# All four channel tiles of a width-31 convolution as packed matmuls, and the memory's transposes one at a time

## The reference

```python
h = rmsnorm(x, mix_pre_norm)
u = h @ w_in                             # 1024 -> 3072
u_a, u_b, hq, hk, hv, hg = six parts of 512 columns of u
# conformer_conv: 512 channels, each with its own 31 taps back in time
c = u_a * sigmoid(u_b)
y = depthwise_conv(c, dw_w) + dw_b       # y[t, ch] = sum_w c[t - 30 + w, ch] * dw_w[w, ch] + dw_b[ch]
y_conv = silu(layernorm(y, ln_w, ln_b))  # mean and variance over the 512 channels
# retention: 4 heads of 128, chunks of 128 tokens, rotary on q and k, decay
y_ret = silu(hg) * rmsnorm_per_head(retention(rotary(hq), rotary(hk), hv))
x = x + rmsnorm(concat(y_conv, y_ret) @ w_out, mix_post_norm)
# then a gated feed-forward of width 2816, a gate on a projected input p, and the second block
```

## Time and profile before

| | |
|---|---|
| profiled execution | 929.86 us |
| its span | 928.0 us |
| granted TensorE clock, mean | 0.994 |
| TensorE busy | 901.5 us, 97% |
| its weight loads (beside the matmuls) | 813.9 us, 88% |
| VectorE busy | 663.8 us, 72% |
| ScalarE busy | 506.1 us, 55% |
| GpSimd busy | 304.7 us, 33% |
| moved by DMA | 163.77 MB, mean 176 GB/s |

### The profile page before, as it was taken

The page is one execution under the profiler, slowest core; times in us unless marked ns, Lnnn a source line. Parts: engine busy times, 40 slices in busy tenths (PEclk is TensorE's granted clock), DMA queues, the critical chain, the costliest instruction groups (busy, mean ns, idle before and its releaser), DMA issues.

```text
span 928.0 us, 16426 instructions
## 1 busy us (share of the span) xinstructions
PE 901.5 (97%) x6864; PEld 813.9 (88%) x6864; DVE 663.8 (72%) x834; ACT 506.1 (55%) x746; POOL 304.7 (33%) x115
## 2 busy tenths in 40 slices
PE   7998999999999999999999999999999999999996
PEld 6998986888888878999999998999999788888885
DVE  4999576888884256758878774867656689999622
ACT  6544736554454446755636575555545466666532
POOL 2000000566664420000000004845684156566542
PEclk9999999999999999999999999999999999999999
DMA  9583453655555545445544434533455365555551
GB/s 355 214 252 112 145 208 119 230 192 193 191 182 186 198 160 181 171 153 196 208 138 156 160 100 156 183 137 132 141 188 199 101 240 181 189 194 201 189 181 45
DMA packets 31800, 163.77 MB, mean 176 GB/s; under 512 B 9169, under 2 KB 10977, under 8 KB 13296
## 3 DMA queue, kind: packets, MB, share of 16 engines
q1 hardware_dynamic: 31664, 162.66, 51.0%
q0 software_dynamic: 64, 0.08, 0.0%
HBM read 161.32 MB, written 1.42 MB: 175 GB/s over the span
## 4 chain that ended last, share of the span: by engine, by line
PE 82%; DVE 13%; ACT 3%; issue 1%; DMA 1%; SPq 0%; DVEq 0%; ACTq 0%
PE ring L1629 28%; PE acc L1707 18%; PE acc L1641 9%; PE ring L1641 9%; PE acc L1642 4%; PE ring L1642 4%; DVE w_lo L1079 3%; PE ring L1660 3%; DVE conv_y L1171 3%; PE acc L1887 1%; DVE y L1131 1%; DVE ret_inv L1245 1%; ACT sq L679 1%; DMA gain_mix_pre<-gains 1%; ACT w_hi L673 1%
## 5 line engine op out<-in xcount | busy, mean ns | idle before, releaser
L636 POOL TENSOR_TENSOR w_lo<-raw,w_hi 128x1024 fp32r<-128x1024 f32 x100 | 287.3, 2875 | 590.8 <-ACT w_hi L673 590.7
L673 ACT CAST w_hi<-raw 128x1024 fp32r<-128x1024 f32 x284 | 297.8, 1054 | 314.7 <-PE ring L1629 132.5
L1079 DVE TENSOR_TENSOR w_lo<-raw,w_hi 128x1024 fp32r<-128x1024 f32 x184 | 228.6, 1256 | 107.5 <-ACT w_hi L673 97.4
L1629 PE MATMUL ring<-h,w_hi 128*128 128x256 f32 x1408 | 259.2, 286 | 3.6 <-DVE w_lo L1079 1.9
L1629 PEld LDWEIGHTS ring<-h,w_hi 128*128 128x128 f32 x1408 | 220.9, 193 | 7.8 <-issue 7.3
L1629 PE MATMUL ring<-h,w_lo 128*128 128x256 f32 x704 | 199.9, 284 | 0.8 <-issue 0.8
L1629 PEld LDWEIGHTS ring<-h,w_lo 128*128 128x128 f32 x704 | 135.6, 193 | 0.0
L1641 PE MATMUL acc<-h,w_hi 128*128 128x512 f32 x352 | 124.7, 397 | 0.8 <-DVE h L1137 0.8
L1641 PE MATMUL ring<-h,w_hi 128*128 128x512 f32 x352 | 124.2, 396 | 0.0
L1642 PE MATMUL ring<-h,w_lo 128*128 128x256 f32 x352 | 98.2, 279 | 0.0
L1642 PE MATMUL acc<-h,w_lo 128*128 128x256 f32 x352 | 98.2, 279 | 0.0
(11 more groups left out here) (254 smaller groups left out, 1255.9 us busy)
## 6 DMA issues: line engine op xcount, KB each, us to landing
raw<-wstream SPq DMA_DIRECT2D x142, 1024.0 KB, 4.9
toep_t<-toep SPq DMA_DIRECT2D x16, 96.0 KB, 3.2
u<-uconv SPq DMA_DIRECT2D x4, 284.0 KB, 7.8
x<-x_tok SPq DMA_DIRECT2D x2, 512.0 KB, 5.4
mem<-mem_tok SPq DMA_DIRECT2D x1, 1024.0 KB, 12.0
w_ple<-wproj SPq DMA_DIRECT2D x1, 1024.0 KB, 7.2
out_t<-y SPq DMA_DIRECT2D x4, 256.0 KB, 2.2
decay<-decay_tab SPq DMA_DIRECT2D x1, 768.0 KB, 6.4
```

What stands on the lines that cost most here:

```text
L636: nc.gpsimd.tensor_tensor(w_lo[:, u % UNITS], unit_of_raw(u), as_f32(w_hi[:, u % UNITS]), ALU.subtract).then_inc(lo_ready["pool"], 1)
L673: nc.scalar.copy(w_hi[:, u % UNITS], unit_of_raw(u)).then_inc(hi_ready, 1)
L1079: V.tensor_tensor(w_lo[:, u % UNITS], unit_of_raw(u), as_f32(w_hi[:, u % UNITS]), ALU.subtract).then_inc(lo_ready["dve"], 1)
L1629: last = mm(dst, w[a], src[:, b, kt], start=n == 0 and i == 0, stop=n == kts - 1 and i == 2)
```

## The change

`PACKED` becomes all four tiles. VectorE's taps go. SP stores and reloads all four tiles of `conv_in`, GpSimd builds four weight blocks, TensorE computes four packed tiles, ScalarE copies four. On TensorE the packed tiles move behind value fill 0, and on ScalarE their copies behind that fill's. The four memory turns are placed singly: 0 behind the packed tiles, 1 behind value fill 1, 2 behind gate fill 0, 3 behind gate fill 1. `u4` now lies where `mem_n` is written later, and its buffers make the arena 1 KiB larger. The mean waits for the packed outputs alone.

```diff
-PACKED = (2, 3)
+PACKED = (0, 1, 2, 3)
-ARENA_KIB = 84
+ARENA_KIB = 85
@@ STAGES
-    ("v", 0, 1, 16, "act"), ("mem_x", 0, 2, 0, "dve"), ("v", 1, 1, 16, "act"), ("mem_x", 2, 2, 0, "dve"),
-    ("g", 0, 2, 16, "act"), ("memk", 0, 2, 16, "act"), ("wout", 0, 1, 64, "acc"),
+    ("v", 0, 1, 16, "act"), ("mem_x", 0, 1, 0, "dve"), ("v", 1, 1, 16, "act"), ("mem_x", 1, 1, 0, "dve"),
+    ("g", 0, 1, 16, "act"), ("mem_x", 2, 1, 0, "dve"), ("g", 1, 1, 16, "act"), ("mem_x", 3, 1, 0, "dve"),
+    ("memk", 0, 2, 16, "act"), ("wout", 0, 1, 64, "acc"),
@@ buffers
-        u4 = at(67, "u4", len(PACKED) * 4, UW)
-        w_conv = at(76, "w_conv", len(PACKED), 4 * PACKS, 32)
+        u4 = at(51, "u4", len(PACKED) * 4, UW)
+        w_conv = at(69, "w_conv", len(PACKED), 4 * PACKS, 32)
@@ ScalarE
+            copy_fill("v", 0, v_ret[:, :, 0:256])
             for i, t in enumerate(PACKED):
                 act.wait_ge(packed_conv, i + 1)
                 A(conv_y[:, t], sc[t][:, 0:S], ACT.Identity, bias=col("dw_b", t)).then_inc(packed_out, 1)
             prime(ACT.Sqrt)
-            for j in range(2):
-                copy_fill("v", j, v_ret[:, :, 256 * j:256 * j + 256])
-                turned_hi("mem", 2 * j)
-                turned_hi("mem", 2 * j + 1)
-            act.wait_ge(conv_ready, 2)
+            turned_hi("mem", 0)
+            copy_fill("v", 1, v_ret[:, :, 256:512])
+            turned_hi("mem", 1)
+            act.wait_ge(conv_ready, 1)
             A(sq[:, 0:4], conv_y[:], ACT.Square).then_inc(sq_ready, 1)
             root("ln_var")
             copy_fill("g", 0, g_ret[:, 0:2], ACT.Silu)
-            act.wait_ge(conv_ready, 3)
+            turned_hi("mem", 2)
+            act.wait_ge(conv_ready, 2)
...
             copy_fill("g", 1, g_ret[:, 2:4], ACT.Silu)
             prime(ACT.Sqrt)
+            turned_hi("mem", 3)
@@ VectorE
-            seen, tap_of = [0] * 4, [0, 0, CW, CW]
-            def tap(j):
...
-                ins = V.scalar_tensor_tensor(out=conv_y[:, j], in0=src, scalar=weight, in1=conv_y[:, j],
-                                             op0=ALU.mult, op1=ALU.add)
-                if min(tap_of) == CW:
-                    ins.then_inc(conv_ready, 1)
...
-            tiles_in = [0]
-            def taps(count):
...
                 wait_read(dve, "conv", j)
-                tiles_in[0] = j + 1
-                taps(7)
...
             for j in range(4):
                 feed_behind("qk", j)
-                taps(7)
...
-            for j in range(2):
-                feed_behind("v", j)
-                turned_lo("mem", 2 * j)
-                turned_lo("mem", 2 * j + 1)
-                taps(8)
+            feed_behind("v", 0)
+            turned_lo("mem", 0)
+            feed_behind("v", 1)
+            turned_lo("mem", 1)
...
             feed_behind("g", 0)
+            turned_lo("mem", 2)
...
             feed_behind("g", 1)
+            turned_lo("mem", 3)
@@ TensorE
+            token_pair("v", 0, h)
             pe.wait_ge(w_conv_ready, len(PACKED))
             pe.wait_ge(conv_loaded, 16 * TAPS)
             for i, t in enumerate(PACKED):
                 conv_packed(i, t)
-            for j in range(2):
-                token_pair("v", j, h)
-                turn("mem", 2 * j, y_tok)
-                turn("mem", 2 * j + 1, y_tok)
+            turn("mem", 0, y_tok)
+            token_pair("v", 1, h)
+            turn("mem", 1, y_tok)
             pe.wait_ge(packed_out, len(PACKED))
-            pe.wait_ge(conv_ready, 1)
...
             tile_out(fill[:, 1], h)
+            turn("mem", 2, y_tok)
             pe.wait_ge(rope_ready, 2)
...
             pair("g", 1, h)
+            turn("mem", 3, y_tok)
```

More of the change, by code:

```diff
@@ L1157, in _ @@
             V.tensor_tensor(lb[:, 0], logits, logits, ALU.subtract).then_inc(lb_exp, 1)
-            seen, tap_of = [0] * 4, [0, 0, CW, CW]
-            def tap(j):
[L1163 to L1170, removed]
-                ins = V.scalar_tensor_tensor(out=conv_y[:, j], in0=src, scalar=weight, in1=conv_y[:, j],
-                                             op0=ALU.mult, op1=ALU.add)
-                if min(tap_of) == CW:
-                    ins.then_inc(conv_ready, 1)
-                else:
-                    seen[j] = link(ins)
-            tiles_in = [0]
-            def taps(count):
[L1182 to L1185, removed]
             dve.wait_ge(pad_ready, 1)
```

## The result

The changed kernel took 934.1 us (median of 8 runs, 929.71 to 937.23), the kernel before 930.03 beside it: a ratio of 1.0041, 95% interval 1.0022 to 1.0059, that is 3.8 us more (2.0 to 5.5). A second set on another occasion gave 1.0039 (1.0024 to 1.0054). The change made the kernel slower, by a little under half a per cent. The forecast was 934.7 and +4.84 us.

A forecast was written before the change was run, and what follows sets the result against it. The prediction took TensorE to bound the kernel. Its terms, 7.05 - 0.62 - 0.81 - 1.47 - 0.86 + 1.55 = +4.84 us, added to 929.86, gave 934.7 us, range 931 to 939.

The forecast's parts named there:

- Two more packed tiles: On TensorE: four packed tiles take 14.10 us where two took 7.05, so +7.05 us, with nothing hidden.
- Waits that go: TensorE waits before the packed group, second value fill and mean vanish: -0.62, -0.81 and -1.47 us.
- The packed input: Store and reload over HBM: lands at 65 to 67.6 us, TensorE asks at 69.7; cost 0, up to +3.
- The rival that builds on a late input: TensorE stands before the packed tiles for their input; at +3 us the time is 937.7; chance 0.12.
- From mean to variance: Layer norm on TensorE: distance from mean start to variance start falls from 6.15 to 5.29 us, -0.86.
- The new wait: TensorE waits for turn 3 before the first memory key fill, after the second gate fill: +1.55 us, bounds 0 to 3.
- GpSimd's longer build: Four weight blocks instead of two, from 19.4 to 27 us; VectorE's split beside it done at 26.8; cost 0.
- The conv and qk fills: Eight fills until 64 us: TensorE busy 48.00 of 48.00, its own pace, so removing the taps gains nothing there.
- The rest only moves: After the retention squares: roots, reciprocals and output projection, with its 1.1 us wait for a split, only move.
- a sign of being wrong: After the output projection: a change of time there would contradict the sum, which takes that part to be only moved.
- the taps slowed the matmuls: Rival: without taps, matmuls up to the second value fill win up to 13 ns each, 5.3 us; 929.4 us; chance 0.09.
- The rival without any new wait: No new wait before the memory keys and the variance wait gone too: +2.5 us, 932.4 us; chance 0.13.

The follow-up runs named there:

- the kernel that waits for them: Changed kernel with its four packed tiles moved back ahead of the first value fill; 938.78 us, ratio 1.0112 to the kernel before.
- the two kernels that show it: Changed order with two packed tiles and the taps back, 929.81 us; two packed tiles with queues reordered and the last two waits removed, 923.86 us.

## Why the prediction was right

Point by point, in the order of the sum:

- *Two more packed tiles, +7.05.* Four take 13.95 us, two took 7.05: **+6.90**. That they lie wholly on the path is shown in the stage by computing them twice (+13.81 there, +13.82 at the output projection, counted from the first fill).
- *Waits that go, -0.62, -0.81, -1.47.* The first value fill follows qk at once (61.76, 61.87), the second starts 0.41 us after the turn, the mean 0.43 after the next, with no wait at any of them. All three went whole. A single turn takes 0.41 to 0.44 rather than 0.52, a term that I had left out: four take 1.72 where two pairs took 2.06, **-0.34**.
- *The packed input.* No wait, as said, but the margin was smaller than the 2 to 5 us I gave. The store was issued at 41.87, the loads from 48.98; in the kernel that waits for them (store at 42.02) they let TensorE go at 66.02, and the changed kernel asks at 67.72: 1.7 us. My estimate for the landing, 65 to 67.6, was good at its upper end. With a low start the whole only moves: store at 43.21, loads from 50.57, which by the 16.9 us of the waiting kernel would be in at an estimated 67.5, and TensorE asks at 69.06, an estimated 1.6 us later. So the margin was 1.6 to 1.7 us with either start, and the 5 us rested on the early end of my estimate. The loads do run at half rate: 194 to 203 GB/s at a full share from 56 to 62 us in the kernel without cover. The rival that builds on a late input came out in that kernel alone. By the figure of the Trainium skill ("DMA: Bandwidth & Descriptors", section "Measured (HBM→SBUF, 128 partitions, SWDGE, issued from GpSimd)", 341 GB/s for 1 MB) the 2.27 MB would have landed an estimated 6.7 us after 49, and that kernel would not have waited; it waited 3.8 us, so the figure does not carry over to these rows.
- *From mean to variance, -0.86.* 5.56 us instead of 6.15: **-0.59**. VectorE copied the mean at E+3.07 (E is 87.92, the end of the second value fill) and not at E+2.95, and the variance started at E+5.99 and not E+5.8; the mean itself, after the shorter turn, at E+0.43. The remaining wait is 0.79, forecast 0.8. My count came out 0.1 us short at VectorE's copy and 0.2 at the variance; that these are the signals between the engines, which I hadn't counted, is not shown.
- *The new wait, +1.55.* From the values to the memory keys 4.13 us instead of 2.53: **+1.60**. ScalarE's copy of turn 3 began at G+3.22 (110.61, G is 107.39), as the sum had it, and moving it ahead of the table load removed the wait. So ScalarE's order is its cause, not VectorE's load.
- *GpSimd's longer build, 0.* Two of VectorE's splits beside it took 5.37 us together, where I had allowed 2.1 each, and were through at 28.7 and not 26.8; no fill waited for them, so the term holds, with less room than I gave it.
- *The conv and qk fills, 0.* I took 48.00 busy of 48.00 for TensorE's own pace. It holds nearly for executions with a low start, where the kernels with taps take 0.2 us more (47.86 and 47.84 against 47.63). With a full start TensorE would be there sooner than VectorE's split, which waits behind the taps; the two kernels that show it lost 1.21 and 0.46 us. This benefit of the change is missing from the sum.
- *The rest only moves.* The wait for a split in the output projection is 1.1 before and 1.0 after, and the output projection takes 32.7 us up to the feed-forward in both. Behind that, from the output projection to the end, I had named a change of time as a sign of being wrong. The profiles have 805.4 us before and 804.4 and 802.0 after, and 803.1 to 806.3 in the other kernels with four packed tiles, so single profiles scatter too much to show one or to rule it out.

The terms as measured, 6.90 - 0.62 - 0.81 - 1.47 - 0.34 - 0.59 + 1.60, make +4.67; with the 0.2 under the fills, that is the +4.40 between the two profiles with a low start. The forecast of 4.84 had the mechanism right. Its errors partly cancel: the turns (0.34), the fills (0.2, or more with a full start) and the tiles (0.15) were charged too high, the variance (0.27) and the new wait (0.05) too low. The median of 934.1 beside the forecast of 934.7 is closer than the sum deserves; the ratio says 3.8, a microsecond less than the forecast.

The rival "the taps slowed the matmuls" is refuted: without taps the fills still take 46.13 / 8 = 5.77 us. The rival without any new wait is refuted by the 1.34 us; the version with turn 3 first comes closest to it. The chance of "slower by over 0.5%" was put at 0.50 and of "no more than 0.5%" at 0.44; the ratios, 1.0041 and 1.0039, lie on the second side, with intervals that cross the line.

Why the change cost time though it took 25 us off the second busiest engine: TensorE had lost 4.1 us to all waits of the touched stretch in that profile, and the two extra tiles cost 6.9. The chain of waits gave the taps 3% of the span, 28 us; it could give back no more than the idle time of the engine that bounds the kernel.

## What to carry to other kernels

Before work is moved onto the engine that bounds a kernel, add up that engine's idle time in the stretch: it is the ceiling of the gain as long as that engine's own work stays the same, whatever share the chain of waits gives to the work that is moved. Do it for an execution in which the bounding engine runs at full clock throughout: here a low clock at the start hid a wait. If the engine that is to be relieved has slack on the whole and is late only at one event, move what stands ahead of that event in its queue; here this gave 3.8 us where the packing lost as much. And when a step is moved behind another, count what stands ahead of it there, table loads included.

## What the hardware showed that I had not expected

- A pause of TensorE costs more than itself. After 3.8 us of waiting the next 4 us were granted 0.57 of the clock (1.7 us more for the packed tiles), after 3.4 us 0.60; with matmuls into an unused bank in the pause it stayed at 1.00. After the pauses of up to 1.5 us in the kernel before, the stretches stayed at 1.00; after the 1.84 to 2.14 us before the first fill both are seen (next point).
- The first 4 us of fills are granted about 0.6 in some executions and 1.00 in others of the same kernel (both seen in the changed one; four low and six full starts in the ten profiles). Without taps that is 1.5 us between the fills, with taps 0.3 and 1.0, so one can't simply subtract it: compare profiles with the same start.
- Beside GpSimd's weight building VectorE's splits of 128x1024 took 2.7 us each instead of 1.22 (two in 5.37, from 23.36 us of the changed kernel), and one of GpSimd's four blocks took 2.90 us where the median is 1.92.
- Loads of 1136-byte rows from HBM kept the queues fully busy at about 200 GB/s, where the weight slots that followed them moved at 418.
